# One-hot columns in quarters of TensorE for the modulation sums of a two-block network

## What is computed

```
mod = (silu(c) @ ada_w[l] + ada_b[l]).reshape(b_, N_SUB, 3, D_MODEL)
y = swiglu(modulate(x, mod[:, 0, 0], mod[:, 0, 1]), ffn_w13[l, 0], ffn_w2[l, 0])
x = layer_norm(ALPHA * x + 0.5 * (1 + mod[:, 0, 2])[:, None, :] * y, ln_g[l, 0], ln_b[l, 0])
```

## Time and profile before

| | us |
|---|---|
| three runs | 1902.84, 1906.97, 1910.09 |
| profiled execution, its own time | 1906.4 |
| its span, first to last instruction | 1904.6 |
| TensorE busy in the span | 1831.3 (96%) |
| VectorE, ScalarE, GpSimd busy | 1268.1, 697.1, 132.0 |

### The profile page before, as it was taken

How to read it: one execution, slowest core, us unless ns; L and a number is a source line. 1 busy time by engine, 2 the same in 40 slices (tenths; PEclk the granted TensorE clock), 3 DMA queues, 4 the chain that set the end, 5 groups by cost and what they waited for, 6 DMA issues and landing times.

```text
span 1904.6 us, 31232 instructions
## 1 busy us (share of the span) xinstructions
PE 1831.3 (96%) x13292; PEld 1590.2 (83%) x13292; DVE 1268.1 (67%) x2249; ACT 697.1 (37%) x936; POOL 132.0 (7%) x68
## 2 busy tenths in 40 slices
PE   7999999999999989999999989999999999899997
PEld 5999988877999989998888779999855555656897
DVE  3977655634888677766664448996793778645744
ACT  3433243332633263333342264332421345224453
POOL 0000063300000000001731000000000000000000
PEclk7999999999999999999999999999999999999999
DMA  9777613422577637665326135675163001341102
GB/s 394 309 278 255 263 71 130 197 114 111 202 281 267 246 134 290 230 249 195 120 112 233 56 141 221 260 273 211 58 232 130 22 1 45 121 155 44 45 23 89
DMA packets 47338, 324.27 MB, mean 170 GB/s; under 512 B 4960, under 2 KB 8160, under 8 KB 8416
## 3 DMA queue, kind: packets, MB, share of 16 engines
q1 hardware_dynamic: 47200, 322.28, 44.4%
HBM read 321.21 MB, written 1.05 MB: 169 GB/s over the span
## 4 chain that ended last, share of the span: by engine, by line
PE 90%; DVE 6%; ACT 2%; issue 1%; DMA 1%; SPq 0%; DVEq 0%; ACTq 0%
PE ps L359 89%; ACT wk L1411 2%; PE ps L362 1%; DVE wk L1950 1%; DMA ring<-in_stream_dram 1%; DVE wk L1953 1%; DVE low L1950 1%; DVE wk L1956 1%; DVE xa L1953 0%; DVE xlo L1950 0%; ACT low L1411 0%; DVE tab L1950 0%; DVE small L2423 0%; DVE wk L1959 0%; ACT xa L1411 0%
## 5 line engine op out<-in xcount | busy, mean ns | idle before, releaser
L359 PE MATMUL ps<-xhi,low 128*128 128x256 f32 x1536 | 411.0, 283 | 0.0
L359 PE MATMUL ps<-xa,ring 128*128 128x256 f32 (+1 forms) x1568 | 398.1, 413 | 9.0 <-ACT xa L1411 5.5
L359 PEld LDWEIGHTS ps<-xa,ring 128*128 128x128 f32 x1568 | 296.2, 191 | 98.8 <-issue 58.3
L359 PE MATMUL ps<-xhi,whi_wk 128*128 128x256 f32 x1088 | 306.6, 291 | 13.4 <-ACT xhi L1411 7.4
L1411 ACT ACTIVATE wk<-ps 128x256 f32<-128x256 f32 (+4 forms) x221 | 109.6, 504 | 559.5 <-PE ps L359 483.7
L359 PE MATMUL ps<-xlo,whi_wk 128*128 128x256 f32 x1088 | 297.9, 283 | 0.0
L359 PEld LDWEIGHTS ps<-xhi,low 128*128 128x128 f32 x1536 | 282.3, 190 | 0.1
L1411 ACT ACTIVATE whi_wk<-ring 128x2048 fp32r<-128x2048 f32 x100 | 191.0, 1913 | 191.3 <-DMA ring<-in_stream_dram 100.3
L1956 DVE SCALAR_TENSOR_TENSOR wk<-ring,sc,wk 128x256 f32<-128x256 f32 x576 | 234.1, 480 | 0.0
L1950 DVE TENSOR_TENSOR low<-ring,whi_wk 128x2048 fp32r<-128x2048 f32 x100 | 228.2, 2285 | 0.0
L359 PEld LDWEIGHTS ps<-xhi,whi_wk 128*128 128x128 f32 x1088 | 207.6, 195 | 17.0 <-issue 15.1
(11 more groups left out here) (124 smaller groups left out, 2563.7 us busy)
## 6 DMA issues: line engine op xcount, KB each, us to landing
ring<-in_stream_dram SPq DMA_DIRECT2D x302, 1024.0 KB, 5.7
tab<-in_tab_dram SPq DMA_DIRECT2D x1, 1376.0 KB, 20.2
res<-in_xt_dram SPq DMA_DIRECT2D x1, 1024.0 KB, 20.4
res<-in_ct_dram SPq DMA_DIRECT2D x1, 1024.0 KB, 7.8
out_dram<-wk SPq DMA_DIRECT2D x2, 512.0 KB, 3.0
tab<-in_wg_dram SPq DMA_DIRECT2D x1, 512.0 KB, 7.7
tab<-in_tab_dram SPq DMA_DIRECT2D x1, 256.0 KB, 2.9
cols<-in_cols_dram SPq DMA_DIRECT2D x1, 243.5 KB, 2.6
```

The source lines that it names most:

```text
L359: last[0] = nc.tensor.matmul(o, l, r, start=start, stop=stop, skip_group_check=free)
```

## The change

A sum over partitions is now made the other way round. The 32 weight columns are a window of a new table, zero except for one column of ones. The products move past them, 128 columns at a time. The sums then lie along one row, of 32 rows in one quarter of PSUM bank 7, and the other 31 rows of the window get zeros added. Successive halves of chunks go to successive quarters (`hot_place`). When a batch is complete, VectorE copies the 128 x 128 rows to SBUF (`rows_out`), one matmul with the identity turns them (`mod_turn`), and VectorE reads the columns in a new order. Unchanged are chunks 0 to 7 of m = 0, 2 and 5.

The order changes with it. In FFNs 0, 2 and 3 chunks 8 and 9 are both left at p = 8, 10 at p = 9, 11 at p = 10. The gate of a split FFN is turned at the end of pass 9 and read by VectorE at j = 20. In MLA the reading of `mod` 7 comes behind `q_part(1)`, and TensorE turns ahead of the first `scores`.

```diff
-for _name, _n in [("ident", 128), ("ones", 256), ("blk", 128), ("pairs64", 6 * 64), ("halves", 448),
+for _name, _n in [("ident", 128), ("ones", 256), ("onehot", 64), ("blk", 128), ("pairs64", 6 * 64), ("halves", 448),
...
+        mod_rows = sb("mod_rows", [P, 128])
...
-            if m != 5:
-                return p
-            return p - 2 if 2 <= p < GATE + 2 else None
+            if m == 5:
+                return (p - 2,) if 2 <= p < GATE + 2 else ()
+            return {8: (8, 9), 9: (10,), 10: (11,), 11: ()}.get(p, (p,))
...
+        def hot_batch(m, ch):
+
+
+            if by_rows(m, ch) or m in (2, 5) and ch < GATE:
+                return None
+            if (m, ch) in LATE_MODS:
+                return "mla", 6
+            if m == 7:
+                return "gates", 7
+            return "ffn", m if is_late(m, ch) else m - 1
+
+        def hot_place(m, ch, t, i):
+
+
+            if is_late(m, ch):
+                j = 2 * (ch - GATE) + t
+                return j % 4, 8 + j // 4
+            if m < 6:
+                return (2 * ch + t) % 4, (2 * ch + t) // 4
+            return 2 * t + i, LATE_MODS.index((m, ch)) if (m, ch) in LATE_MODS else ch % GATE
...
+            begun = {}
+
             def mod_cols(m, ch):
 
                 eng.wait_ge(*step_of("modsum", m, ch))
                 n = 1 if m < 6 else 2
-                if ch == 0 and m:
+                batch = hot_batch(m, ch)
+                quarters = begun.setdefault(batch, set())
+                if batch is None and ch == 0 and m:
                     eng.wait_ge(vector_done, step("mod", m - 1))
-                late = 32 if is_late(m, ch) else 0
+                elif batch is not None and not quarters:
+                    eng.wait_ge(vector_done, step("mod", batch[1]))
                 for t in range(2):
                     for i in range(n):
-                        c = (2 * ch + t) * n + i + late
-                        mm(bank(7, c, c + 1), mod_sum(m, ch, i)[:, P * t:P * t + P], ones[:, 0:1], True, True)
+                        data = mod_sum(m, ch, i)[:, P * t:P * t + P]
+                        if batch is None:
+                            mm(bank(7, 2 * ch + t, 2 * ch + t + 1), data, ones[:, 0:1], True, True)
+                        else:
+                            g, r = hot_place(m, ch, t, i)
+                            mm(PS[32 * g:32 * g + 32, 7, 0:P], table("onehot", 31 - r, 32), data, g not in quarters, True, free=True)
+                            quarters.add(g)
...
+            def mod_turn(name, o, start=True):
+
+                eng.wait_ge(vector_done, step("modrows", *name))
+                mm(o, mod_rows[:, :], ident, start, True, free=True)
...
+                    if m in SPLIT_MODS and p == 9:
+                        mod_turn(("gates", m), bank(7, P, 2 * P), False)
+                    if m in SPLIT_MODS and p == 10:
+                        eng.wait_ge(vector_done, step("gate", m))
...
-                if m % 3 != 1 and m != 5:
-                    mod_cols(m + 1, 11)
+                if m % 3 != 1:
+                    mod_turn(("mod", m + 1), bank(7, 0, P))
...
-                eng.wait_ge(vector_done, step("mod", 7))
+                mod_turn(("mod", 7), bank(7, 0, P))
                 eng.wait_ge(scalar_done, step("k_rope"))
...
                 unit(lambda k: w[:, k, 0:P], True, False)
+                mod_turn(("gates", 7), bank(7, 0, P))
                 unit(lambda k: w[:, k, P:T], True, True)
                 gates(0)
...
+            def rows_out(name, final):
+
+
+                eng.wait_ge(tensor_done, step("modcol", *final))
+                copy(mod_rows[:, :], bank(7, 0, P), "modrows", *name).then_inc(vector_done, 1)
...
                 eng.wait_ge(tensor_done, step("accb", m, 0))
-                if m in SPLIT_MODS:
-                    gate(m)
...
+                if m % 3 != 1:
+                    rows_out(("mod", m + 1), (m + 1, GATE - 1 if m == 5 else 11))
                 eng.wait_ge(tensor_done, step("mu", m))
...
+                    if kind == "w13" and j == 18 and m in SPLIT_MODS:
+                        rows_out(("gates", m), (m, 11))
+                    if kind == "w13" and j == 20 and m in SPLIT_MODS:
+                        gate(m)
...
-                if ada_of(m, 11) is not None:
-                    mod_part(m + 1, 11)
                 norm(m)
...
-                late_gate(6)
-                modulation(7)
...
                 q_part(0)
+                rows_out(("mod", 7), LATE_MODS[-1])
                 q_part(1)
+                late_gate(6)
+                modulation(7)
...
-                late_gate(7)
+                rows_out(("gates", 7), (7, 11))
                 eng.wait_ge(tensor_done, step("in2", m, 0))
                 copy(a_r, bank(0), "in2_read", m, 0).then_inc(vector_done, 1)
+                late_gate(7)
...
+    put("onehot", np.tile(np.arange(64) == 31, (P, 1)))
```

More of the change, by code:

```diff
@@ L414, in mod_cols @@
                     found["chunk", found["chunk_no", "ada", m, ch][1]] = found["modcol", m, ch]
-                if ch == 11:
-                    found["modps", m] = found["modcol", m, ch]
+            def mod_turn(name, o, start=True):
+                eng.wait_ge(vector_done, step("modrows", *name))
+                mm(o, mod_rows[:, :], ident, start, True, free=True)
+                last[0].then_inc(tensor_done, 1)
+                done.named("modturn", *name)
             def ffn(l, f):
@@ L488, in ffn @@
                         found["down", m, j] = found["down", m, j - 1] = found["chunk", held[0]]
-                    if ada_of(m, p) is not None:
-                        leave("ada", m + 1, ada_of(m, p))
+                    for ch in ada_of(m, p):
+                        leave("ada", m + 1, ch)
                     if p and late_ada(m, p - 1):
                         mod_cols(m, late_ada(m, p - 1))
-                    if p and ada_of(m, p - 1) is not None:
-                        mod_cols(m + 1, ada_of(m, p - 1))
+                    if m in SPLIT_MODS and p == 9:
+                        mod_turn(("gates", m), bank(7, P, 2 * P), False)
+                    if m in SPLIT_MODS and p == 10:
+                        eng.wait_ge(vector_done, step("gate", m))
+                    for ch in (ada_of(m, p - 1) if p else ()):
+                        mod_cols(m + 1, ch)
                 found["acc", m] = found["accb", m, 3] = found["down", m, FT - 1]
@@ L938, in turned @@
                     eng.wait_ge(vector_done, step("pn", h))
+                    if h == 0:
+                        eng.wait_ge(vector_done, step("mod", 7))
                     if h:
@@ L1204, in gates @@
                     eng.wait_ge(*step_of("in2_read", m, 0))
+                    eng.wait_ge(vector_done, step("gate", 7))
                     if d:
@@ L1994, in gate, with both_vectors @@
                 eng.wait_ge(vector_done, done.count)
-                tt(mod[:, m % 2, 16:24], bank(7, 48, 56), col("ada_b", 24 * m + 16, 8), ADD, "gate", m).then_inc(vector_done, 1)
+                tt(tiles(mod[:, m % 2, 16:24], 4), turned_out(bank(7, P, 2 * P))[:, 8:10], tiles(col("ada_b", 24 * m + 16, 8), 4), ADD, "gate", m).then_inc(vector_done, 1)
                 eng.wait_ge(vector_done, done.count)
                 ts(aux[:, m % 2, 8:16], mod[:, m % 2, 16:24], 1.0, ADD, 0.5, MUL).then_inc(vector_done, 1)
+            def both_vectors(o, r, bias):
+                rows, n = turned_out(bank(7, 0, P))[:, r:r + o.shape[1] // 4], bias.shape[1] // 2
+                return o.rearrange("p (r t i) -> p r t i", t=2, i=2), rows.rearrange("p r (t i) -> p r t i", i=2), \
+                    bias.rearrange("p (r t) -> p r t", t=2).unsqueeze(3).to_broadcast([P, n, 2, 2])
@@ L1999, in late_gate @@
             def late_gate(m):
-                eng.wait_ge(tensor_done, step("modcol", 7, GATE - 1 if m == 6 else 11))
+                eng.wait_ge(tensor_done, step("modturn", *(("mod", 7) if m == 6 else ("gates", 7))))
                 eng.wait_ge(vector_done, done.count)
-                tt(tiles(mod[:, m % 2, 32:48], 2), tiles(bank(7, 32, 48), 2), each(col("ada_b2", 24 * (m - 6) + 16, 8), 2), ADD, "gate", m).then_inc(vector_done, 1)
+                tt(*both_vectors(mod[:, m % 2, 32:48], 0, col("ada_b2", 24 * (m - 6) + 16, 8)), ADD, "gate", m).then_inc(vector_done, 1)
@@ L2021, in modulation @@
                     eng.wait_ge(vector_done, done.count)
-                    tt(o[:, 0:24], bank(7, 0, 24), col("ada_b", 24 * m, 24), ADD, "mod", m).then_inc(vector_done, 1)
+                    tt(tiles(o[:, 0:24], 4), turned_out(bank(7, 0, P))[:, 0:6], tiles(col("ada_b", 24 * m, 24), 4), ADD, "mod", m).then_inc(vector_done, 1)
                     eng.wait_ge(vector_done, done.count)
@@ L2032, in modulation @@
                     eng.wait_ge(vector_done, done.count)
```

(8 more changed lines are left out.)

11 lines of the change are left out of this document (5 added, 6 removed).

## The result

The changed kernel takes 1894.5 us in the median of six runs (1890.71 to 1896.97), the kernel before 1911.84 in six runs (1902.84 to 1914.86): a ratio of 0.9914, interval 0.9889 to 0.9939. Timed a second time it took 1894.28 against 1907.78, 0.9926 (0.9907 to 0.9944). So the medians are 13 to 17 us lower (0.7 to 0.9%), and both lie within the forecast of 1891 (1886 to 1902). The profiled execution took 1890.71 us, 15.7 less than that of before.

A forecast was written before the change was run, and what follows sets the result against it. TensorE, busy 96% of the span, was taken as the bound. Cheaper sums -12.0, FFN ends -2.7 and MLA's first scores -0.9 gave -15.6 us, from 1906.4 to 1890.8, stated as 1891, range 1886 to 1902.

The forecast's parts named there:

- The bound: TensorE, busy 96% of the span: a microsecond off its sequence is one off the result; VectorE counts only where TensorE waits.
- Quarters run side by side: In every changed group, records in different quarters overlap; a round, one record in each quarter in use, costs 0.11 us.
- serial rival: In every group quarters take turns, records costing 0.11 us one by one: +27.9 us, 1918.7, slower by 0.6%; chance 0.08.
- rival of loads in the path: Each of 130 rounds pays an unhidden weight load of 0.11 us: +14.3 us, 1905.1, no change; chance 0.09.
- The streams: Cheaper modulation sums inside the FFNs, MLA and y2 on TensorE: together -12.0 us over 51 groups.
- a double: FFN 0 and 2, passes 2 and 6: a late and a next chunk together on four different quarters, -0.39 us each.
- dearer return: Each of 42 FFN groups pays 0.11 us more going back: +4.6 us, 1895.4, or 1900 if paid twice; chance 0.09.
- The ends: At the ends of FFN 0 and FFN 2, reading the gate earlier removes TensorE's wait of 1.34 us each, -2.7 together.
- rival of the ends that stay: Residual tiles, the turning or `q_part(1)` still hold TensorE, so only the -12.0 counts: 1894.4 us; chance 0.06.
- MLA's first scores: Between MLA's last pair and first scores, VectorE's idle time of 1.08 us goes, less 0.22 for the turning: -0.9 us.
- Costed at nothing: Six PSUM copies (at most 2.6 us uncovered), chunk 9's products in pass 8, the gate wait at p = 10: 0 us.
- The sum: Whole kernel: -12.0 - 2.7 - 0.9 = -15.6 us, from 1906.4 to 1890.8 profiled, stated as 1891.

The follow-up runs named there:

- one-quarter run: Changed kernel with both halves of an FFN chunk of m < 6 summed in the same quarter, four rounds instead of two: 1903.74 us, ratio 0.9973.
- order-only run: Kernel before with only the new order of chunks, gate and `mod` reads, sums still one-column matmuls: 1904.89 us, ratio 0.9977 to the kernel before.
- its reverse: Changed kernel with the gates of FFN 0, 2 and 5 read behind the FFN's last modulation group: 1897.47 us, ratio 0.994 to the kernel before.
- paired version: Changed kernel with modulation chunks of m + 1 in FFN 0, 2 and 3 summed two at a time: 1889.23 us (0.9898), again 1888.97 (0.9902).

## Why the prediction was right

- **The bound.** That a microsecond out of TensorE's sequence is one of the result held: the steps sum to 13.2 us, and the medians fell by 17.3 and 13.5.
- **Quarters run side by side; a round costs 0.11.** Shown by the one-quarter run, and by 0.34 and 0.35 us for four and eight records. The serial rival is out. So is the rival of loads in the path: four rounds, each with loads of 0.108, fit in 0.57 us with the way back. By the rule of the Trainium skill (TensorE: Matmul & The Clock Gate, Part 3, "The mechanism"), that a load overlaps running matmuls only in other rows, it would have been the forecast; these quarters share all rows, and the trace disagrees for 128 columns as it did for 256. That section of the Trainium skill also names a background weight buffer, into which a load can go ahead of running matmuls; the prediction left this out, and it would permit what the trace shows.
- **The streams** were the mis-sized term: -9.6 us instead of -12.0, nearly all of it in the FFNs (-2.0 instead of -4.1). A single chunk in an FFN costs 0.09 us more than before, not 0.05, a double saves 0.35, not 0.39, and 12 records save 0.58, not 0.61. The lead (0.21) and the group itself (0.34) came as worked out. What I had left out is that the first ordinary record behind a group takes 0.02 more to the next one than it did behind a one-column group (0.22 for 0.20). The rest of the 0.04 is rounding of both prices (0.55 for 0.54 after, 0.48 for 0.49 before), on a pattern that occurs 42 times, about 1.7 us. Some 0.4 more comes from ordinary records, 118.8 to 118.9 ns apart in the changed kernel and 118.7 to 118.8 before. The 0.02 are the dearer return in kind, at a fifth of the 0.11 that the rival gave it.
- **The ends.** -1.28 each, of the 1.34 taken; both the order-only run (-1.35, -1.37) and its reverse (+1.18 twice, FFN 5 unchanged) put it down to the gate's reading. The rival of the ends that stay is out.
- **MLA's first scores.** -1.07 for -0.9. "1.08 less the turning's 0.22" took the idle time behind the end of a record. From start to start it was 1.67 us where such records come every 0.43, so 1.24, and 1.24 less 0.22 is 1.02. What the old order of reads would have cost behind the turning the prediction didn't ask: 3.3 us of idle time and about 5 in all.
- **Costed at nothing**: the row copies, chunk 9's products in pass 8, the wait for the gate at p = 10. No step and no idle row of TensorE stands at any of them. The count was wrong: there are nine copies, not six, of 0.28 us each.
- **The sum** hit 1890.8 to 0.1 us in the profiled execution, and that is luck: 2.4 us too much in the streams met about 2.5 of clock. The medians, 1894.5 and 1894.3, lie about a microsecond above what 1906.4 - 13.2 = 1893.2 gives.

Open are two things: what in the operands' place sets the distance of FFN records (three places were seen, and which tensor's place counts was not tried), and what makes the late half-clock stretches come or stay away.

## What to carry to other kernels

Price a small side job inside a stream of large matmuls by start-to-start distance, from the last ordinary record ahead of it to the second one behind it, less the two ordinary distances in between. On quarters that comes here to a fixed part of 0.31 us and 0.11 for each round (0.53 for two rounds, 0.75 for four). On the whole array it is 0.11 a record with no fixed part (0.45 for four). If the fixed part leads, fill the quarters and collect jobs before going there: two chunks at once cost what one did, and this took the medians down by 5 us more. When a new step (here the turning) goes ahead of a read, look at what is queued behind that read on its engine. And before a difference under half a per cent is credited to an edit, compare records whose code didn't change: the clock and the place of the buffers moved them by up to 0.4%.

## What I had not expected of the hardware

- A working area moved by 384 bytes a partition (640 in the kernel before) brought the ordinary FFN records 1.0 to 1.2% closer together (118.7 to 118.9 ns before, 117.5 after), at the same granted clock: 6.8 us of steps in the kernel before, whose median fell by 4.0, and 7.0 in the paired version's median.
- Short half-clock stretches, most of them worth up to 1.7 us and the longer ones 3.3, come and go in the same code: the same late program, started 3.5 us later, differed by 5.9 us for that, and two profiles of one program by 3.0. Behind 3.3 us of idle time ahead of MLA's first scores such a stretch came in both profiles; behind 1.08, or none, in no profile.
- A one-hot window of 128 columns as weights costs no more than a column of ones as moving data: 0.36 us for four records in either form.
